# First differential attention of a two-block model on one core: maxima scaled on ScalarE, Square moved ahead of the second exponential, two peak reductions taken into the loop

## The reference

```python
def _diff_attention(q1, q2, k1, k2, v, lam):
    ...
        def probs(qb, k):
            s = jnp.einsum('bhqd,bshd->bhqs', qb, k).astype(jnp.float32) * scale
            return jax.nn.softmax(jnp.where(mask, s, -jnp.inf), axis=-1)
        a = probs(qb1, k1) - lam * probs(qb2, k2)
        return jnp.einsum('bhqs,bshe->bhqe', a.astype(v.dtype), v)
...
    o = _rms(o, subln) * (1.0 - lambda_init)
    o = o.reshape(b, s, DA_V) * jax.nn.silu(g)
    return x + o @ w_out
```

## Time and profile before

| | us |
|---|---|
| median of 3 runs | 2532.23 |
| lowest, highest | 2521.53, 2538.52 |
| the profiled execution, its own time | 2530.41 |
| its span in the trace | 2528.6 |
| of it the first attention, from the first scores to the last groups | 1416 to 1650 |
| busy in the whole span: PE, DVE, ACT, POOL | 2363.5, 1519.4, 968.2, 216.0 |
| busy in 1416.06 to 1650: PE, DVE, ACT | 179.3, 200.2, 161.5 of 233.9 |

### The profile page before, as it was taken

One profiled execution on the slowest core, in us unless ns is written; L12 is line 12 of the kernel. 1 busy time (PEld: TensorE's weight loads), 2 busy tenths in 40 slices (PEclk: granted clock), 3 DMA queues, 4 the chain that ended last, 5 costly groups with the idle time before them and its releaser, 6 DMA issues.

```text
span 2528.6 us, 30214 instructions
## 1 busy us (share of the span) xinstructions
PE 2363.5 (93%) x12840; PEld 1252.4 (50%) x12840; DVE 1519.4 (60%) x1962; ACT 968.2 (38%) x1383; POOL 216.0 (9%) x263
## 2 busy tenths in 40 slices
PE   6999999999999999898999777899999998888899
PEld 4445444444444444344444455654444445666764
DVE  6898755644454455777631488965534307888862
ACT  5245334212121212323321466732323116777741
POOL 0001030000000002324201101022000000000000
PEclk9999999999999999898999899999999998999999
DMA  4010011110101010121011000021130100000021
GB/s 177 34 67 34 1 34 63 70 67 34 67 34 67 34 67 34 36 101 67 34 67 34 1 1 1 8 93 34 67 133 34 68 1 34 1 1 1 1 84 50
DMA packets 50326, 116.00 MB, mean 46 GB/s; under 512 B 2386, under 2 KB 7819, under 8 KB 49808
## 3 DMA queue, kind: packets, MB, share of 16 engines
q1 hardware_dynamic: 48456, 105.40, 11.8%
q10 hardware_dynamic: 1736, 8.68, 0.8%
HBM read 101.49 MB, written 12.58 MB: 45 GB/s over the span
## 4 chain that ended last, share of the span: by engine, by line
PE 76%; DVE 13%; ACT 6%; issue 3%; DMA 1%; POOL 1%; ACTq 0%; DVEq 0%; POOLq 0%
PE PS L72 72%; ACT RG L81 4%; PE PS L75 3%; DVE R L93 2%; DVE R L101 2%; DVE RG L107 2%; DVE mx L110 2%; DVE RG L101 2%; ACT OV L84 1%; DVE scl L110 1%; DMA RG<-in_a_w_in 1%; DVE RG L93 1%; DVE oss L110 1%; ACT R L81 1%; ACT OV L81 0%
## 5 line engine op out<-in xcount | busy, mean ns | idle before, releaser
L72 PE MATMUL PS<-R,RG 128*128 128x512 f16 (+1 forms) x5472 | 1167.6, 375 | 10.2 <-DVE RG L101 4.7
L72 PEld LDWEIGHTS PS<-R,RG 128*128 128x128 f16 (+1 forms) x5472 | 543.4, 103 | 631.8 <-issue 14.5
L72 PE MATMUL PS<-RG,R 128*128 128x512 f16 x2880 | 634.6, 381 | 4.5 <-DVE R L101 4.0
L72 PEld LDWEIGHTS PS<-RG,R 128*128 128x128 f16 x2880 | 282.7, 98 | 337.8 <-issue 7.5
L81 ACT ACTIVATE R<-PS,scl 128x512 f32<-128x512 f32 (+1 forms) x192 | 126.8, 687 | 716.1 <-PE PS L72 616.3
L101 DVE SCALAR_TENSOR_TENSOR R<-PS,scl,R 128x512 f32<-128x512 f32 (+1 forms) x208 | 148.7, 746 | 149.2 <-PE PS L72 124.1
L107 DVE TENSOR_TENSOR_SCAN RG<-RG 128x127 f32<-128x127 f32 (+7 forms) x128 | 168.6, 1345 | 110.4 <-ACT RG L81 110.1
L72 PE MATMUL PS<-R,OV 128*128 128x64 f32 (+2 forms) x1456 | 194.5, 286 | 34.9 <-DVE R L93 32.8
L101 DVE SCALAR_TENSOR_TENSOR RG<-RG,scl 128x4096 f16<-128x4096 f32 (+1 forms) x43 | 188.7, 4389 | 52.2 <-ACT RG L81 52.2
L72 PEld LDWEIGHTS PS<-R,OV 128*128 128x128 f32 x1456 | 180.6, 199 | 45.1 <-DVE R L93 39.3
L75 PE MATMUL PS<-ident,RG 128*128 128x128 f32 x864 | 148.5, 289 | 47.1 <-ACT OV L84 23.9
(11 more groups left out here) (120 smaller groups left out, 1546.7 us busy)
## 6 DMA issues: line engine op xcount, KB each, us to landing
RG<-in_w_ff SPq DMA_DIRECT2D x16, 2048.0 KB, 8.1
RG<-in_a_w_in SPq DMA_DIRECT2D x8, 2048.0 KB, 8.5
RG<-in_w_in SPq DMA_DIRECT2D x4, 2048.0 KB, 9.6
xspill<-R ACTq DMA_DIRECT2D x2, 4096.0 KB, 15.3
RG<-in_w_kv SPq DMA_DIRECT2D x4, 2048.0 KB, 8.0
RG<-in_b_w_in SPq DMA_DIRECT2D x4, 2048.0 KB, 7.9
R<-in_x SPq DMA_DIRECT2D x8, 512.0 KB, 9.1
RG<-in_w_out SPq DMA_DIRECT2D x2, 2048.0 KB, 7.7
```

The lines of the kernel that those rows point to most:

```text
L72: return self.engine.matmul(*a, **k) if self.engine else Nothing()
```

## The change

Three edits, all in the first attention.

1. `top` loses the multiplication by `ssc` and the wait ahead of it. ACT does it: a Copy with scale `ssc`, in place on `mx`, ahead of the exponential of side 0 (once for both sides below group 22, for each side from it on), and a wait of ACT for its own result.
2. On ACT the Square at a block's end, and the waits for it, stand ahead of the exponential of side 1 in its turn, no longer behind.
3. The peak of gate tile 7 and the maximum of the eight move from ahead of the loop to the end of DVE's turn 3. The peak of weight tile 31 is taken in four pieces of 1024 columns at the end of turns 8 to 11, and their maximum in turn 12.

```diff
@@ vector, ahead of the loop
+            def gate_peak(t):
+                e.wait_ge(*sig("gg_gain").at(t))
+                e.tensor_reduce(col(32 + t), GG[:, t, :], AX.X, ALU.max, apply_absolute_value=True).then_inc(*step.up())
+
...
-                e.wait_ge(*sig("gg_gain").at(t))
-                e.tensor_reduce(col(32 + t), GG[:, t, :], AX.X, ALU.max, apply_absolute_value=True).then_inc(*step.up())
-            e.wait_ge(*step.last())
-            e.tensor_reduce(col(123), col(32, 8), AX.X, ALU.max).then_inc(*sig("o_peak").up())
-            measure(31)
+                if t < NT - 1:
+                    gate_peak(t)
@@ vector, top
-                e.tensor_reduce(out, z, AX.X, ALU.max, negate=True).then_inc(*step.up())
-                e.wait_ge(*step.last())
-                e.tensor_scalar(m, m, ssc, None, ALU.mult).then_inc(*sig("top_a").up(u, sides[-1]))
+                e.tensor_reduce(out, z, AX.X, ALU.max, negate=True).then_inc(*sig("top_a").up(u, sides[-1]))
@@ vector, the loop over u
+                if u == 3:
+                    gate_peak(NT - 1)
+                    e.wait_ge(*step.last())
+                    e.tensor_reduce(col(123), col(32, 8), AX.X, ALU.max).then_inc(*sig("o_peak").up())
+                if 8 <= u < 12:
+                    j = u - 8
+                    e.wait_ge(*sig("raw").at(31))
+                    e.tensor_reduce(col(112 + j), w_raw(31)[:, 1024 * j:1024 * j + 1024], AX.X, ALU.max,
+                                    apply_absolute_value=True).then_inc(*step.up())
+                if u == 12:
+                    e.wait_ge(*step.last())
+                    e.tensor_reduce(w_col(31, 0), col(112, 4), AX.X, ALU.max).then_inc(*sig("w_peak").up(31))
@@ scalar, exp(u, c)
+                if c == 0 or u >= da_first:
+                    m = da_scale(u, c)
+                    m = mx[:, m:m + len(hs) * (1 if u >= da_first else 2)]
+                    e.wait_ge(*sig("constants").at("ssc"))
+                    e.activation(m, m, ACT.Copy, scale=ssc).then_inc(*sig("top_scaled").up(u, c))
+                    e.wait_ge(*sig("top_scaled").at(u, c))
@@ scalar, the loop over u
-                if u < N:
-                    exp(u, 1)
                 if 3 <= u < N + 3 and da_groups[u - 3][1][-1] % 4 == 3:
...
                     e.activation(sqb, bo, ACT.Square).then_inc(*sig("o_square").up(i, g))
+                if u < N:
+                    exp(u, 1)
```

More of the change, by code:

```diff
@@ L1575, in top @@
                 e.wait_ge(*full.at("za", u, sides[-1]))
-                e.tensor_reduce(out, z, AX.X, ALU.max, negate=True).then_inc(*step.up())
-                e.wait_ge(*step.last())
-                e.tensor_scalar(m, m, ssc, None, ALU.mult).then_inc(*sig("top_a").up(u, sides[-1]))
+                e.tensor_reduce(out, z, AX.X, ALU.max, negate=True).then_inc(*sig("top_a").up(u, sides[-1]))
             N = len(da_groups)
-            e.wait_ge(*sig("constants").at("ssc"))
             for u in range(N + 4):
```

## The result

| | before | changed |
|---|---|---|
| median of 20 runs, us | 2531.26 (2521.53 to 2545.39) | 2517.3 (2510.49 to 2530.3) |
| profiled execution, us | 2530.41 | 2523.40 |
| its span, us | 2528.6 | 2521.6 |
| its loop: first mask product to the table load behind it, us | 244.89 | 229.30 |

The ratio is 0.9942 [0.9928, 0.9956]: 14 us less than before, between 11 and 18. So I compare the loops alone, by marks on the timeline: the start of PE's first mask product, of the `top` of each turn, and of ACT's table load behind the last turn. "Turn u" is from one `top(u)` to the next.

What follows compares the result with a forecast made beforehand. A ring of PE scores, DVE `top` and ACT exponential, no engine full, bounds the attention loop. Terms -6.1+0+2.7-1.2+4.0-1.0-6.6 sum to -8.2 us: 2522.2 profiled, 2524 us forecast, chance 0.60, range 2512 to 2535.

Steps and rivals of the forecast that it cites:

- turn 28: Eighth block's end at i=4 to 7: no gain, DVE behind anyway beside POOL; table load covered, else it costs 1.3 us.
- i=3: Turns at i=3: two blocks' ends give -1.4 us, 0.2 given back for full engines; net -1.2 us.
- ordinary turns: Turns at i=4 to 7 outside blocks' ends: Copy costs +4.0 us; lighter DVE in turns 29, 31 and 32 gives -1.0.
- i=2: Turns at i=2: the weight's peak pieces cost 4.0 us, two blocks' ends give back 1.3; net +2.7 us.
- The start: Mask product to first exponential: peaks gone, Copy 0.30 us and exposed table load 1.28 us paid; gain 6.1 us.
- Groups 0 to 6: Turns at i=0 and 1: Copies +1.0, turn 3's gate peak +1.35, earlier Squares -2.3 us; sum 0.
- the turns stay at 2.1: At i=2: DVE needs 1.86 us a turn, PE about 2.05, ACT 2.15, so turns keep their length.
- Ordinary turns of 2.5 us stay: At i=3: PE's work 2.5 us and ACT's 2.46 keep turns outside blocks' ends at their length.
- Blocks' ends: At i=4 to 7: the earlier Square and lighter DVE shorten seven of eight ends, -6.6 us in all.
- A: Rival: ACT nearly full at i=3 to 5, gains at blocks' ends (6.6 and 1.2 us) go; 2532 us, chance 0.17.
- C: Rival: Copy with ACT's wait for itself costs 0.6 us in each of 54 rings; 2540 us, chance 0.08.
- B: Rival: pieces in DVE waits 2 us, less slow clock at start 1, Copy at 0.23 3.8; 2518 us, chance 0.15.

Runs made afterwards that it cites:

- The run with the load early: Changed kernel plus a one-column exponential on ACT ahead of the wait for `top` in turns 0 and 28; loop 229.09 us, ratio to before 0.9925.
- the doubled scaling: Changed kernel plus a second one-column ACT Copy and a wait for it behind each scaling; loop 245.88 us, ratio to before 1.0014.
- one delay: Changed kernel plus one 128x128 reduction, result unused, on DVE ahead of the factor of turn 53; loop 229.14 us.

## Why the prediction was right or wrong

The time was inside the range, and every term that had a sign had the right one; the sum was 7.4 us too small, and 6.1 of that lies in four terms: turn 28, the end, i=3 and the ordinary turns. At i=2 and in the ordinary turns two errors within a term cancel in part; there it is luck that the term fits as well as it does.

- **The start**, 6.1 of 6.1: the Copy at 0.30, the table load exposed, nothing paid behind it. The run with the load early priced it, 1.3 at the start. The drain that the Trainium skill ("ScalarE: Activation LUTs", section "What ACT_TABLE_LOAD costs") would add did not appear at the loads of this loop: exponentials that wait for nothing else follow by 0.01 to 0.05 us.
- **Groups 0 to 6**, -0.4 for 0. The three edits alone moved this stretch by +1.1 (scaling), +1.5 (peaks) and -2.7 (squares), for +1.0, +1.35 and -2.3 in the sum.
- **i=2**, +2.15 for +2.7, with turns 9 to 11 at 2.97 for a forecast 3.0. The pieces cost 4.05 for 4.0 (21.69 against 17.64 in the run of scaling and squares). But "the turns stay at 2.1" failed: turns 7 and 13, which have no piece, fell from 2.10 to 1.84 and 1.85, and the two blocks' ends gave back 0.9 in that run for the 1.3 forecast. These two errors cancel in part.
- **i=3**, -2.3 for -1.2. The step "Ordinary turns of 2.5 us stay" failed. Four of the six went from 2.50 to between 2.24 and 2.31 (turns 14 and 18 stayed at 2.37 and 2.70), and the 0.2 for full engines was not due. The 2.5 us of PE were a mean over the stretch, blocks' ends included. In turn 17, before and then changed, DVE sets the pace and PE and ACT have room:

```profile
1484.00:1486.50 2.50, 1.67 (x15) 0.83 (x13) 2.39 (x6) 0.99 (x3) 0.00 (x0) 1.00 0.00 0
```
```profile
1478.17:1480.41 2.24, 1.68 (x15) 0.84 (x13) 2.17 (x5) 0.96 (x2) 0.00 (x0) 1.00 0.00 0
```

- **Ordinary turns**, +1.9 for +3.0. At i=6 and 7 0.08 each, as from the exchange of 0.21 for 0.30; at i=5 0.08 for 0.20, at i=4 0.20 for 0.33. I had held ACT's copy of the transposes fixed. It starts 0.77 us behind the mask product, before 0.89 in most turns, since the transposes wait for DVE's join, and DVE is lighter. So the +4.0 came out as 2.1. The -1.0 for a lighter DVE in turns 29 to 32 came out as -0.2 (turns 29 to 31, where 29 scatters by 0.4): both were too large, and in the sum they cancel in part.
- **Blocks' ends**, -6.9 for -6.6: the Square ahead and a DVE with two multiplications less, as forecast, turn by turn within 0.1 us. What the text did not say is that it takes both: alone, each edit did 0.4 us worse in such a turn than I then expected (5.61 for 5.2, 6.66 for 6.2).
- **Turn 28**, -1.85 for 0. The step was "DVE is behind anyway". It was behind because it met POOL badly, and the two multiplications that it lost moved it to a better place. Over turns 28 to 31 the gain is 2.0 (20.1 to 18.1). The load's cover held.
- **The end**, -2.1 for 0. The text put nothing there, with no row for it and no reason. DVE's two multiplications less shortened PE's gap from 2.51 to 1.82, which gave 0.7, and 1.4 came from the clock.

Of the rivals, A (full ACT eats the Squares) fell: ACT was busy 26.5 of 30 us from 1570 to 1600 and the blocks' ends gained all the same, at i=3 and 4 too (4.32 us in turn 16 for 4.93, 4.24 in turn 24 for 4.92). C fell with the Copy at 0.30 and a wait of 0.02; the doubled scaling shows that its rule, so much for each of some 50 rings, was right. B had the right side for other reasons: not the weight's pieces in waits, not a Copy of 0.23, but turn 28, a lighter DVE at i=3, and at the end 1.4 us of clock; whether the slow clock at the start gave back its 1 us no run separates. What misled me most was to price the scaling as a loss on ACT, with little given back for DVE. In the ordinary turns of i=4 to 7 it is that loss. But where DVE sets the pace, at i=2 and 3, at blocks' ends once the Square stands ahead, and at the loop's end, it is a gain.

## What to carry to other kernels

Price an edit against the path that the other edits leave, not the path of before: what takes work off engine X is worth nothing, or less, until another edit has made X the last to arrive. Short instructions of one engine that run beside long ones of another should be looked at for the moment at which they start, and a gap of PE for what the clock does behind it; both can give more or less than the edit moves. Work moved into a wait takes with it everything that its result feeds on other engines. The mean busy time of a stretch does not say which engine sets the pace of a turn in it; the turn by itself does. And a difference between two traces is worth something only when it is larger than that between two traces of the same code.

## What the runs showed of the hardware that I had not expected

**A DVE instruction beside POOL's.** A factor of 128x1 took 0.22 us alone and from 0.48 to 1.95 (0.49, 0.86, 1.12, 1.71, 1.79, 1.85) when it met one of POOL's products of 1.90 us, and always ended with it; a join of 128x640 took 2.48 or 2.49 for 0.89. Reductions over PSUM in the same stretch took their usual time (two of 128x640 in 1.54 us). The waiting goes both ways: the product that follows took 2.48 us. I have not shown which resource they share.

**The same code in 864 or 876 us.** What lies behind the loop is equal in all fourteen kernels. In the profiled executions it took 864.0 to 864.8 us in seven, 867.4 (before) and 869.1 in two, and 875.9 to 877.4 in five (the changed kernel 876.6). The granted clock differs in the second attention; busy time from 2100 to 2300 us, changed kernel and then that with one delay:

```profile
2100.00:2300.00 200.00, 171.43 (x1371) 135.31 (x1365) 159.09 (x142) 139.15 (x213) 7.51 (x6) 0.87 0.03 12
```
```profile
2100.00:2300.00 200.00, 169.79 (x1453) 134.65 (x1452) 168.26 (x145) 147.16 (x226) 7.25 (x5) 0.93 0.03 12
```

PE is busy as long in both, but at 0.87 it gets through 1371 matmuls, at 0.93 through 1453. This alone makes 13 of the 20 to 24 us by which runs of one kernel differ, and it is why a gain of 15 us in a loop can show as 7 in one pair of spans. What decides it at a given execution stays open.
